# Chunks of h at multiples of 64 bytes, and another order of the three products of a weight block

## The reference

```python
def norm_mod(h, j):                      # h, the input of a sublayer
    return _rms(h) * g_norm[l, j] * (1.0 + scale) + shift
def _swiglu(h, w_up, w_down):            # w_up 1024 x 5632, w_down 2816 x 1024
    g, u = jnp.split(h @ w_up, 2, axis=-1)
    return (jax.nn.silu(g) * u) @ w_down
x = x + 0.5 * gate(0) * _swiglu(norm_mod(x, 0), w_ffn_up[l, 0], w_ffn_down[l, 0])
...
bias = t5_table[t5_bucket(k_pos - q_pos)]   # in one attention of the second mixer kind
```

## Time and profile before

| | |
|---|---|
| median of three runs | 1713.06 us |
| the profiled execution, its own time | 1709.39 us |
| its span, first to last instruction | 1707.6 us |
| mean granted clock of TensorE, share of full speed | 0.984 |
| TensorE busy | 1635.3 us (96%), 13290 matmuls |
| VectorE busy | 1313.3 us (77%) |
| ScalarE busy | 913.9 us (54%) |
| moved from and to DRAM | 403.22 MB, mean 236 GB/s |

### The profile page before, as it was taken

The page is one execution under the profiler, slowest core; times in us unless marked ns, Lnnn a source line. Parts: engine busy times, 40 slices in busy tenths (PEclk is TensorE's granted clock), DMA queues, the critical chain, the costliest instruction groups (busy, mean ns, idle before and its releaser), DMA issues.

```text
span 1707.6 us, 31946 instructions
## 1 busy us (share of the span) xinstructions
PE 1635.3 (96%) x13290; PEld 1604.8 (94%) x13290; DVE 1313.3 (77%) x2071; ACT 913.9 (54%) x1564; POOL 84.0 (5%) x124
## 2 busy tenths in 40 slices
PE   2999999999999999999999999979999999899998
PEld 2999998999999999998999999978999998899998
DVE  6688898788788878897788888847888898385553
ACT  5445458664445544477554545646545456464453
POOL 4000000000000000000110001001000010010000
PEclk8999999999999999999999999989999999999999
DMA  9787765348786778754378888313778773145451
GB/s 357 301 317 300 300 253 198 124 178 336 294 317 261 300 300 316 290 210 173 115 271 312 305 318 301 124 50 117 301 300 319 296 250 124 50 149 197 176 196 50
DMA packets 57168, 403.22 MB, mean 236 GB/s; under 512 B 6606, under 2 KB 6866, under 8 KB 9280
## 3 DMA queue, kind: packets, MB, share of 16 engines
q1 hardware_dynamic: 55424, 396.01, 61.6%
q0 software_dynamic: 1600, 5.18, 1.0%
HBM read 400.10 MB, written 1.05 MB: 235 GB/s over the span
## 4 chain that ended last, share of the span: by engine, by line
PE 81%; DVE 11%; ACT 4%; issue 2%; DMA 1%; SPq 0%; DVEq 0%; ACTq 0%
PE PS L507 81%; DVE WL L1602 3%; DVE SCR L1602 2%; DVE SCR L1605 1%; ACT WH L1146 1%; DVE ring L1629 1%; ACT SCR L1429 1%; DMA SCR<-in_x 1%; DVE X L1605 1%; DVE HL L1605 1%; DVE SCR L1599 1%; DVE SMALL L1984 1%; DMA ring<-in_win 0%; ACT HH L1178 0%; DVE SCR L1946 0%
## 5 line engine op out<-in xcount | busy, mean ns | idle before, releaser
L1602 DVE TENSOR_TENSOR WL<-ring,WH 128x1024 fp32r<-128x1024 f32 (+1 forms) x508 | 599.8, 1215 | 187.4 <-ACT WH L1146 186.8
L507 PE MATMUL PS<-HH,WH 128*128 128x256 f32 (+1 forms) x2640 | 651.5, 285 | 12.7 <-ACT WH L1146 9.5
L507 PE MATMUL PS<-HL,WH 128*128 128x256 f32 (+1 forms) x2640 | 640.1, 283 | 0.0
L1146 ACT ACTIVATE WH<-ring 128x1024 fp32r<-128x1024 f32 (+1 forms) x508 | 510.9, 1048 | 100.1 <-PE PS L507 39.7
L507 PEld LDWEIGHTS PS<-HH,WH 128*128 128x128 f32 x2640 | 497.2, 190 | 18.8 <-ACT WH L1146 9.7
L507 PEld LDWEIGHTS PS<-HL,WH 128*128 128x128 f32 x2640 | 495.1, 190 | 0.7
L507 PE MATMUL PS<-HH,WL 128*128 128x256 f32 (+1 forms) x2640 | 375.9, 280 | 2.3 <-DVE WL L1602 2.2
L507 PEld LDWEIGHTS PS<-HH,WL 128*128 128x128 f32 x2640 | 339.4, 189 | 3.7 <-DVE WL L1602 3.7
L1629 DVE CUSTOM_DVE_ANT_0 ring<-ring,CB,VC 128x1024 f32<-128x1024 f32 x240 | 316.4, 1339 | 9.0 <-DMA ring<-in_ada 8.9
L507 PE MATMUL PS<-AH,WH 128*128 128x256 f32 x1056 | 297.5, 282 | 0.0
L507 PE MATMUL PS<-AL,WH 128*128 128x256 f32 x1056 | 297.0, 281 | 0.0
(11 more groups left out here) (206 smaller groups left out, 1488.0 us busy)
## 6 DMA issues: line engine op xcount, KB each, us to landing
ring<-in_up SPq DMA_DIRECT2D x88, 1024.0 KB, 5.6
ring<-in_ada SPq DMA_DIRECT2D x72, 1024.0 KB, 7.2
ring<-in_ffn SPq DMA_DIRECT2D x66, 1024.0 KB, 4.8
ring<-in_mod SPq DMA_DIRECT2D x48, 1024.0 KB, 6.9
ring<-in_down SPq DMA_DIRECT2D x44, 1024.0 KB, 6.5
ring<-in_win SPq DMA_DIRECT2D x32, 1024.0 KB, 6.9
ring<-in_wout SPq DMA_DIRECT2D x16, 1024.0 KB, 4.8
ring<-in_winv SPq DMA_DIRECT2D x4, 1024.0 KB, 4.8
```

Of the source, the lines that this page charges most:

```text
L507: return e.matmul(out, lhsT, rhs, start=start, stop=stop, skip_group_check=skip)
L1146: e.activation(half_of(i)[0], slot_of(("unit", u))[:, w * (i % 2):w * (i % 2) + w], ACT.Copy).then_inc(s_hi, 1)
L1602: return e.tensor_tensor(out, a, b, op)
```

## The change

HH and HL get 272 columns per chunk (1088 bytes) instead of 258; the products of `early` read 258 of them as before. To make room, the one-hot constant (320 columns) and the table go, with the product and the copy that used them: the small array `t5rel` now comes with the inputs, laid out from the table on the host.

The plain halves of the up projection in sublayers 2, 3, 5, 7 and 9 wait for `s_hi` and `s_lo` and then issue the same 24 products in an order given by `UP_ORDER`, another for each of the five. The down projection takes its three products of a block in an order given by `DOWN_ORDER`, per sublayer; the first and the last sublayer keep the old one. The wait for `s_lo` stands ahead of the first product that reads WL. In the tuples, (w, h, k) is WH or WL, HH or HL, and the chunk.

```diff
-              ("cnt", 512), ("causal", 128), ("nones", 128), ("chunk", 256), ("sbpos", 128), ("sb01", 128),
-              ("onehot", 320)]
+              ("cnt", 512), ("causal", 128), ("nones", 128), ("chunk", 256), ("sbpos", 128), ("sb01", 128)]
...
-VEC_SPEC = [("gfinal", 8), ("t5", 4), ("lam", 8)]
+VEC_SPEC = [("gfinal", 8), ("lam", 8)]
...
+UP_ORDER = ([(0, 0, k) for k in range(8)] + [(0, 1, k) for k in range(8)] + [(1, 0, k) for k in range(8)],
+            [(w, h, k) for k in range(8) for w, h in ((0, 0), (0, 1), (1, 0))],
+            [(w, h, k) for k in range(8) for w, h in ((0, 0), (1, 0), (0, 1))],
+            [(w, 0, k) for k in range(8) for w in range(2)] + [(0, 1, k) for k in range(8)],
+            [(0, 1, k) for k in range(8)] + [(w, 0, k) for k in range(8) for w in range(2)])
+DOWN_ORDER = (((0, 1), (0, 0), (1, 0)), ((0, 0), (1, 0), (0, 1)), ((1, 0), (0, 0), (0, 1)), ((0, 1), (1, 0), (0, 0)), ((0, 0), (0, 1), (1, 0)))
...
-        HH = sb("HH", [128, KD, S + 2], F32R)
-        HL = sb("HL", [128, KD, S + 2], F32R)
+
+        HH = sb("HH", [128, KD, 272], F32R)
+        HL = sb("HL", [128, KD, 272], F32R)
...
-                    e.wait_ge(s_t5c, 1)
-                    e.dma_start(A["t5rel"], SW2[0:4, 0:320]).then_inc(s_t5, 16)
-                    e.wait_ge(s_t5, 16)
...
                 e.wait_ge(s_hi, i + 1)
+                if not first and n in (2, 3, 5, 7, 9):
+                    e.wait_ge(s_lo, i + 1)
+                    for j, (w, h, k) in enumerate(UP_ORDER[(2, 3, 5, 7, 9).index(n)]):
+                        last = mm(out, (wh, wl)[w][:, k, :], (HH, HL)[h][:, k, 0:S], start=j == 0, stop=j == 3 * KD - 1)
+                    last.then_inc(s_half, 1)
+                    return
...
-                    mm(out, wh[:, g, :], xh(k), start=k == 0, stop=False)
-                    mm(out, wh[:, g, :], xl(k), start=False, stop=False)
-                    if g == 0:
-                        e.wait_ge(s_lo, h + 1)
-                    last = mm(out, wl[:, g, :], xh(k), start=False, stop=k == kt - 1)
+                    order = DOWN_ORDER[(2, 3, 5, 7, 9).index(n)] if n else DOWN_ORDER[4]
+                    for j, (w, x) in enumerate(order):
+                        if g == 0 and w == 1:
+                            e.wait_ge(s_lo, h + 1)
+                        last = mm(out, (wh, wl)[w][:, g, :], (xh, xl)[x](k), start=k == 0 and j == 0, stop=k == kt - 1 and j == 2)
...
-                if n == 4:
-                    e.wait_ge(s_xp, 8 * MIX_AT[n] + 8)
-                    bias_of_distance()
...
-                if n == 4:
-                    e.wait_ge(s_t5mm, 1)
-                    e.wait_ge(s_x, 8 * n + 8)
-                    e.tensor_copy(SW2[0:4, 0:320], PS[0:4, 7, 0:320]).then_inc(s_t5c, 1)
...
-    v[0:32, VEC["t5"]:VEC["t5"] + 4] = a["t5_table_2"]
+    out["t5rel"] = np.ascontiguousarray(a["t5_table_2"][buckets()].T)
```

More of the change, by code:

```diff
@@ L121, in build @@
         s_gates, s_mlaw, s_poolw = sem("s_gates"), sem("s_mlaw"), sem("s_poolw")
-        s_t5, s_toe_sa, s_toe_ca, s_out = sem("s_t5"), sem("s_toe_sa"), sem("s_toe_ca"), sem("s_out")
+        s_toe_sa, s_toe_ca, s_out = sem("s_toe_sa"), sem("s_toe_ca"), sem("s_out")
         s_hi, s_lo, s_half = sem("s_hi"), sem("s_lo"), sem("s_half")
@@ L160, in build @@
         s_mq, s_mk, s_mv, s_mkv, s_mlamask, s_zcak = (sem("s_" + k) for k in ("mq", "mk", "mv", "mkv", "mlamask", "zcak"))
-        s_t5mm, s_t5c, s_pmix, s_poolmm = (sem("s_" + k) for k in ("t5mm", "t5c", "pmix", "poolmm"))
+        s_pmix, s_poolmm = sem("s_pmix"), sem("s_poolmm")
         s_o, s_oss, s_od, s_ot, s_oh, s_ol = (sem("s_" + k) for k in ("o", "oss", "od", "ot", "oh", "ol"))
@@ L549, in early @@
                     for k in range(KD):
-                        mm(out, wh[:, k, :], HH[:, k, :], start=k == 0, stop=False)
-                        mm(out, wh[:, k, :], HL[:, k, :], start=False, stop=False)
-                        mm(out, wl[:, k, :], HH[:, k, :], start=False, stop=k == KD - 1).then_inc(s_free if k < KD - 1 else s_half, 1)
+                        mm(out, wh[:, k, :], HH[:, k, 0:S + 2], start=k == 0, stop=False)
+                        mm(out, wh[:, k, :], HL[:, k, 0:S + 2], start=False, stop=False)
+                        mm(out, wl[:, k, :], HH[:, k, 0:S + 2], start=False, stop=k == KD - 1).then_inc(s_free if k < KD - 1 else s_half, 1)
                     return
@@ L557, in early @@
                         e.wait_ge(s_yl, 8 * (n - 1) + k + 1)
-                    mm(out, wh[:, k, :], HH[:, k, :], start=k == 0, stop=False)
-                    mm(out, wh[:, k, :], HL[:, k, :], start=False, stop=False)
+                    mm(out, wh[:, k, :], HH[:, k, 0:S + 2], start=k == 0, stop=False)
+                    mm(out, wh[:, k, :], HL[:, k, 0:S + 2], start=False, stop=False)
                 e.wait_ge(s_lo, i + 1)
                 for k in range(last_chunk):
-                    last = mm(out, wl[:, k, :], HH[:, k, :], start=False, stop=k == KD - 1)
+                    last = mm(out, wl[:, k, :], HH[:, k, 0:S + 2], start=False, stop=k == KD - 1)
                 if p == 0:
@@ L566, in early @@
                     e.wait_ge(s_yl, 8 * n)
-                    mm(out, wh[:, k, :], HH[:, k, :], start=False, stop=False)
-                    mm(out, wh[:, k, :], HL[:, k, :], start=False, stop=False)
-                    last = mm(out, wl[:, k, :], HH[:, k, :], start=False, stop=True)
+                    mm(out, wh[:, k, :], HH[:, k, 0:S + 2], start=False, stop=False)
+                    mm(out, wh[:, k, :], HL[:, k, 0:S + 2], start=False, stop=False)
+                    last = mm(out, wl[:, k, :], HH[:, k, 0:S + 2], start=False, stop=True)
                 last.then_inc(s_half, 1)
@@ L860, in mixer1 @@
                 out_round(n, 1, {})
-            def bias_of_distance():
-                mm(PS[0:4, 7, 0:320], VC[0:32, VEC["t5"]:VEC["t5"] + 4], const("onehot", None, 32)).then_inc(s_t5mm, 1)
             def mixer2(n):
@@ L2195, in constants, with buckets @@
     put("one", np.ones((128, 1)))
+    return c
+def buckets():
     rel = -(np.arange(320) - 63)
@@ L2199, in constants @@
     large = 8 + (np.log(nf / np.float32(8)) / np.float32(np.log(16.0)) * np.float32(8)).astype(np.int32)
[L2200 to L2204, removed]
+    return np.where(rel > 0, 16, 0) + np.where(n < 8, n, np.minimum(large, 15))
 def lay_out(a):
@@ L2317, in program @@
         A[name] = nc.dram_tensor("in_" + name, x.shape, F32, kind="ExternalInput").ap()
-    A["t5rel"] = nc.dram_tensor("t5rel", (4, 320), F32, kind="Internal").ap()
     A["out"] = nc.dram_tensor("out", (256, 1024), F32, kind="ExternalOutput").ap()
```

## The result

The kernel before took 1713.91 us (median of 4 runs, 1709.82 to 1714.86), the changed one 1700.37 us (4 runs, 1696.22 to 1701.73). The ratio is 0.9922, 95% interval 0.991 to 0.9934: 13.5 us faster. Forecast were 34.

The account below looks back on a forecast made before the run. TensorE's product cadence was taken as the bound; 19.0 + 10.2 - 2.0 + 3.6 + 2.7 + 0.3 = 33.8 us off gave a median of 1679 us, from 1713.1. Range 1666 to 1711, the forecast case's own 1666 to 1688.

Parts of the forecast that it names:

- What bounds the kernel: Whole kernel: TensorE's matmuls hold 81% of the chain, so time is number of products times cadence, and the seams.
- the term of 19.0 us for the up projection: Five later up projections: aligned chunks settle into the fast cadence, 4.4 us less 0.6 each, 19.0 us saved.
- Down projection: Down projections of five later sublayers: 2.35 us saved in each of four, 0.85 in the last, 10.2 us.
- 2.0 given back: Waits for weights in down projections: faster products eat into the loads' lead, 0.5 us in four sublayers.
- First sublayer: Old orders, only aligned chunks: 7.2 us saved or nothing, as it settles fast or not; middle 3.6 taken.
- Mixers: About 12 halves of each of four read h with 256 columns: 5.4 us saved or nothing; 2.7 taken.
- Bias of distance: Seam where the dropped product, copy, store and reload stood: 0 to 0.7 us saved, 0.3 taken.
- The WL wait: Start of later up projections: sixth half waits for weight remainders and the next can't run ahead, 0.6 us lost per sublayer.
- (b): Rival, chance 0.17: alignment buys nothing, streams still settle in 117.8 ns; about 1 us off, 1712.
- (c): Rival, chance 0.08: with HH and HL aligned, reads meet at every product, 125 ns; +32 us, 1745.
- (a): Rival, chance 0.25: only some stretches settle fast, two or three of five later sublayers; 21 us off, 1692.

Follow-up runs that it names:

- layout_only: Changed kernel with both old product orders back, keeping 272 columns and the bias from the host; 1697.56 us, ratio 0.9928.
- ah_64_on: Changed kernel with AH, AL, YH and YL moved 64 bytes on, to distance 0 from the weights; 1716.95 us in one run.
- dense: Changed kernel with 256 columns per chunk, old orders and the two shift columns left out, so not the whole work; 1706.37 us, one run.
- orders_only: Changed kernel with 258 columns per chunk again, keeping the new orders and the bias from the host; 1710.68 us, ratio 1.0005.
- dense_pad128: As dense, with 128 unused bytes ahead of WH and all that follows; 1699.48 us, one run.
- wide288_pad64: Changed kernel with 288 columns per chunk, old orders, 64 unused bytes ahead of WH and one buffer of c; 1689.35 us, one run.
- wide320_pad192: As wide320_pad64 but with 192 unused bytes instead of 64, so h stands 64 bytes after the weight blocks; 1696.55 us, ratio 0.9902.
- neither: Changed kernel with 258 columns and the old orders, so only the bias of distance comes from the host; 1710.48 us, ratio 1.0.
- wide320_pad64: Changed kernel with 320 columns per chunk, old orders, 64 unused bytes ahead of WH and one buffer of c; 1683.97 us, ratio 0.9826.
- extra8: wide320_pad64 plus eight extra products at distance 0 ahead of each sublayer's ninth half; 1710.32 us, ratio 0.9986.
- extra2: wide320_pad64 plus two extra products at distance 0 ahead of each sublayer's ninth half; 1707.26 us, ratio 0.997.

## Why the prediction was wrong

**What bounds the kernel** was right: the products' cadence, 272 against 283 cycles of the 2.4 GHz clock (113.3 and 117.8 ns at a granted clock of 1.00), and nothing else moved the profiled time by more than the 3.2 us of the mixers.

**The step that failed** is the reading behind the term of 19.0 us for the up projection: "a stream with aligned chunks can settle into either cadence". AH and AL, the only aligned streams of the trace, were aligned and also at one fixed distance from the weight blocks; I put down to the first what belongs to the second. Chunks 1088 bytes apart start at multiples of 64 bytes, but their distance modulo 256 runs through 0, 64, 128 and 192. The runs give 2.880 us for 0, 2.845 to 2.852 for 128, 2.720 or 2.827 for 64 on either side; the mean of the four with the slow one is (2.880 + 2.848 + 2 x 2.827) / 4 = 2.846, near the 2.840 measured. That sum was made afterwards, and single products don't follow it: over 30 halves of the changed kernel's first sublayer, the product behind WH x HH of chunk 0 starts 117 ns later and that behind chunk 4 122 ns, though both chunks are at distance 0. So how the mixture comes to 2.840 isn't shown. What is shown is that none of the 18 up projections with the 1088-byte step (the changed kernel, layout_only, ah_64_on) ran at 2.720, and that with one kept distance of 64 some did. In place of 19.0 us the up projections of the later sublayers lost 1.3 (190 halves), and the first sublayer lost 0.25 in its up projection.

**Down projection**: 10.2 us less 2.0 given back were forecast. The later sublayers gave 2.33 x 3 + 1.65 + 0.87 = 9.5, with only one long WL wait in mid down projection (sublayer 7, 0.7 us). The size was right partly by luck, since half of the reason was not: I had the fast cadence entered from a fast up projection. In the changed kernel it is entered from a slow one. AH and AL kept their distance, and their cadence still changed in all six sublayers; with 258 columns it is mostly slow (two turned fast in orders_only), with 272 fast in the changed kernel and in layout_only, and fast too behind the up projections of dense, dense_pad128 and wide288_pad64, 30 of 30 in all. So the stream ahead of it bears on the state that the down projection starts in. It doesn't settle it alone: in wide320_pad192 three down projections turned fast and three stayed slow behind up projections of the same 2.827. How it acts isn't shown.

**First sublayer**: I took 3.6, half of all or nothing. It was its down projection, 2.06, and not the up projection. **Mixers**: 2.7 forecast, 3.2 measured, and that is luck, because its parts go with the clock and not with the columns. In sublayer 4 of before, and in sublayer 1 of the changed kernel, a stretch of the output product ran at the lower clock of 1.2 GHz; in the mixer of sublayer 8 such stretches took more of the time before. TensorE's windows of before, the low stretch in sublayer 4 and the mixer of sublayer 8:

```profile
827.20:830.40 3.20, 3.20 (x17) 0.50 0.27 110
1365.00:1505.00 140.00, 129.09 (x965) 0.95 0.40 141
```

and of the changed kernel, in sublayer 1 and again in sublayer 8:

```profile
329.80:333.00 3.20, 3.20 (x17) 0.50 0.28 115
1357.00:1496.00 139.00, 127.38 (x970) 0.98 0.42 145
```

The 24 products that the low stretch falls in take 4.9 us instead of 3.3. In sublayer 4 of before it begins just behind a wait of 1.8 us for VectorE; neither has the same wait there, 1.8 us, and no low stretch. Sublayer 4 got 2.2 us shorter and sublayer 1 1.2 longer; in neither, with 258 columns and no low stretch at these places, both take 118.2. Sublayer 8 got 1.8 us shorter, with 6.8 us at the low clock (by the trace's clock records) where it had 13.7; with the 272 columns of layout_only and 13.7 us low it takes 141.2, against 141.3 before. So no run shows that the mixers gained from the columns. YH's cadence is drawn too: the last four halves of the output product of sublayer 1 took 11.3 us and now take 10.9, but 10.9 in neither as well, and those of sublayer 4 took 10.9 already. The 1.0 us at the start isn't of the change either: the first product starts at 34.7 us before, at 35.7 in the changed kernel and at 34.8 in layout_only. **Bias of distance**: neither shows 0, with bounds of 2 us. **The WL wait**: 0.6 us a sublayer forecast; the wait ahead of the sixth half and what follows it cost 0.24 to 0.28, by the comparison with layout_only.

**The rivals.** (b) came closest for the up projection, though with the sign turned (1.5 us lost from the seventh halves on, where it gave 1.4 gained), and not for the down projection. (c) named a slow case that exists: products whose operands start at one place modulo 256 take 2.880 us a half, in dense and ah_64_on. That their reads meet isn't shown. The 1088-byte step comes to that place only at every fourth chunk, and its price is 120.0 ns, not the 125 I took from chunk 3. (a), only some stretches fast, was the closest in its result (1692), but the stretches were chosen by projection, not by chance.

The Trainium skill ("SBUF — State Buffer", the section on the DMA port swizzle) speaks of lines of 16 bytes; by that, moving h or AH by 64 bytes changes nothing. ah_64_on took 1716.95 us for it, the changed kernel 1700.37, so lines of 16 bytes can't be the cause. The gap of 262 cycles (the Trainium skill, "TensorE: Matmul & The Clock Gate", Back-to-back issue gap), which the section gives for an isolated product, appears in no run here; the fastest is 272.

**Still open**: what picks 2.720 or 2.827 at a distance of 64 bytes. Shown is that it changes at a gap, a handover or a foreign product, differs between sublayers with the same code, and then holds. That it differs between runs of one kernel is inferred from the spread of wide320_pad64. Whether some start always gives the fast one wasn't found. That the place counts modulo 256 fits all kernels here, but apart from the 1032-byte step only distances in steps of 64 were tried. dense, its two variants, wide288_pad64 and ah_64_on rest on one run each; their cadences were read in some 38 halves of each sublayer.

## What to carry to other kernels

When a row shows that one code runs at two speeds, list everything in which the fast place differs from the slow one before naming one of them; "aligned" was true of the AH stream, and so was "always the same distance from the weights". In a kernel bound by TensorE, the start addresses of the two operands against each other are a parameter like a tile size: give each moving chunk one distance of 64 bytes from its weight block modulo 256, on either side (0 and 128 never ran fast here), and check by the count of products in a window. And where a kernel's runs spread wider than its neighbours', look for a state that is drawn per stretch, and compare windows rather than totals; the clock column of such a window tells whether a stretch was shorter for another reason.

## What the runs showed of the hardware

For fp32r products of 256 columns with 128 x 128 weights, back to back, clock 1.00, from one start to the next by the distance of the moving chunk's start from the weight block's modulo 256 bytes: 0 gives 120.0 ns (dense, ah_64_on); 128 gives 118.5 to 118.8 (dense_pad128); 64 on either side gives 113.3 or 117.8, two states; a run through all four gives 118.3 (the changed kernel, layout_only), and 117.5 in one sublayer of ah_64_on. Unaligned chunks 1032 bytes apart give 118.1 on average, and 118.8 to 119.7 in the later sublayers of orders_only and sublayer 2 of neither. The distances are added up from the buffers' sizes. The states hold for 60 halves and more, some 165 us, pass from one projection into the next, and eight or even two foreign products at distance 0 threw every fast stream into the slow one (six of six in extra8, three of three in extra2, one profiled execution each).
